# Prompt attention with 64-feature heads: key rows stacked in high and low parts, and scores in two passes in place of three

## What is computed

```python
# FoX: F is the running sum of the log forget gates
s = einsum('bqhd,bkhd->bhqk', q, k) * 64 ** -0.5
s = s + F_q[..., :, None] - F_k[..., None, :]
s = where(kpos <= qpos, s, NEG_INF)
y = einsum('bhqk,bkhd->bqhd', softmax(s), v)
# SWA: bands of two chunks, with ALiBi and a sink
s = einsum('bcqngd,bcknd->bcngqk', q, k) * 64 ** -0.5 - slopes * dist
y = sink_softmax(s, sink) @ v
```

## Time and profile before

| | us |
|---|---|
| median of 3 runs | 3229.61 (3228.44 to 3230.09) |
| the profiled execution | 3231.43 |
| its span, first to last instruction | 3229.7 |
| TensorE products busy | 2960.0 (92%) |
| TensorE weight loads busy | 2770.8 (86%) |
| VectorE busy | 1578.2 (49%) |
| ScalarE busy | 999.4 (31%) |
| GpSimd busy | 919.6 (28%) |
| mean granted TensorE clock | 0.938 of full speed |

### The profile page before, as it was taken

One profiled execution on the slowest core, in us unless ns is written; L12 is line 12 of the kernel. 1 busy time (PEld: TensorE's weight loads), 2 busy tenths in 40 slices (PEclk: granted clock), 3 DMA queues, 4 the chain that ended last, 5 costly groups with the idle time before them and its releaser, 6 DMA issues. The chain is left out here.

```text
span 3229.7 us, 51941 instructions
## 1 busy us (share of the span) xinstructions
PE 2960.0 (92%) x20656; PEld 2770.8 (86%) x20656; DVE 1578.2 (49%) x2747; ACT 999.4 (31%) x2259; POOL 919.6 (28%) x538
## 2 busy tenths in 40 slices
PE   6998877689999999999999998776899999999998
PEld 6997755379999999999999975645699999999998
DVE  3336555763344444444452574657443444444443
ACT  4334435553311111111243263455343111111111
POOL 3112134133422322322231123332243322223220
PEclk9998968798999999999999998787899999999999
DMA  5120100003411111111211201000133111111111
GB/s 162 39 68 23 40 11 18 1 14 100 153 40 52 46 45 39 52 39 42 69 65 38 77 2 41 11 18 1 34 120 126 52 39 39 52 39 52 39 52 55
DMA packets 181253, 161.86 MB, mean 50 GB/s; under 512 B 17236, under 2 KB 168316, under 8 KB 180860
## 3 DMA queue, kind: packets, MB, share of 16 engines
q1 hardware_dynamic: 181116, 160.02, 15.8%
HBM read 129.97 MB, written 30.13 MB: 50 GB/s over the span
## 5 line engine op out<-in xcount | busy, mean ns | idle before, releaser
L2059 PE MATMUL bank_b<-x_hi,fwhi 128*128 128x352 f32 x2112 | 689.3, 326 | 5.3 <-POOL fwlo L2015 5.3
L2059 PE MATMUL bank_b<-x_hi,fwlo 128*128 128x352 f32 x2112 | 687.5, 326 | 0.0
L2059 PE MATMUL bank_b<-f_lo,fwhi 128*128 128x352 f32 x2112 | 685.9, 325 | 0.0
L2015 POOL TENSOR_TENSOR fwlo<-raw,fwhi 128x1024 fp32r<-128x1024 f32 x132 | 321.8, 2438 | 578.7 <-ACT fwhi L2140 568.2
L2059 PEld LDWEIGHTS bank_b<-x_hi,fwhi 128*128 128x128 f32 x2112 | 398.8, 189 | 6.6 <-POOL fwlo L2015 5.9
L2059 PEld LDWEIGHTS bank_b<-f_lo,fwhi 128*128 128x128 f32 x2112 | 401.1, 190 | 0.0
L2059 PEld LDWEIGHTS bank_b<-x_hi,fwlo 128*128 128x128 f32 x2112 | 397.8, 188 | 0.6
L2248 DVE TENSOR_TENSOR fx<-fx,bank_b 128x352 f32<-128x352 f32 x528 | 275.8, 522 | 242.6 <-PE bank_b L2089 242.6
L2089 PE MATMUL bank_b<-fuhi,fwhi 128*128 128x352 f32 x1056 | 343.8, 326 | 4.5 <-DVE fulo L2242 4.5
L2089 PE MATMUL bank_b<-fulo,fwhi 128*128 128x352 f32 x1056 | 345.3, 327 | 0.0
L2089 PE MATMUL bank_b<-fuhi,fwlo 128*128 128x352 f32 x1056 | 344.7, 326 | 0.0
(11 more groups left out here) (428 smaller groups left out, 6025.6 us busy)
## 6 DMA issues: line engine op xcount, KB each, us to landing
raw<-in_w_ffn_up SPq DMA_DIRECT2D x88, 512.0 KB, 3.8
raw<-in_w_ffn_down SPq DMA_DIRECT2D x44, 512.0 KB, 3.5
wraw<-in_w_in SPq DMA_DIRECT2D x18, 984.0 KB, 5.4
xs<-x_between SPq DMA_DIRECT2D x16, 528.0 KB, 3.9
x_between<-xs SPq DMA_DIRECT2D x16, 528.0 KB, 2.7
fx<-x_between SPq DMA_DIRECT2D x2, 4224.0 KB, 12.5
raw<-in_w_out SPq DMA_DIRECT2D x16, 512.0 KB, 5.3
x_between<-fx SPq DMA_DIRECT2D x3, 1408.0 KB, 5.7
```

Source lines behind the costliest of these rows:

```text
L2015: pool.tensor_tensor(self.wlo[:, r], self.raw[:, o % 2], self.whi[:, r].bitcast(F32), ALU.subtract)\
L2059: last = pe.matmul(bank[:, first_bank + t, 0:TN], w[:, role, c, :], x[:, c, self.cols(t)], start=(c == 0 and m == 0), stop=(c == DC - 1 an ...
```

## The change

For 64-feature heads the high queries are stored twice, in rows 0 to 63 and 64 to 127 of `qT[0]`, and the keys' high part in rows 0 to 63 and low part in rows 64 to 127 of `kT[0]`. The first pass contracts over 128 rows: high query x high key plus high query x low key. The second takes the low queries with the high keys, over 64 rows in SWA and 66 in FoX. In FoX it needs the high keys a second time, in `kT[1]`, whose rows 64 and 65 take the high and low part of -F; rows 64 and 65 of the low queries are 1. ScalarE makes the extra copies: of the queries in both kinds, of the keys in FoX. The zero rows and their memsets and waits go; one GpSimd memset of ones stays in FoX. MLA (96 features) keeps three passes. In SWA `kT` has one array in place of two.

```diff
-        qT = [T("qT" + n, [96, RQ, 2, P], F32R) for n in ("hi", "lo")]
-        kT = [T("kT" + n, [96, 2, 2, SEQ], F32R) for n in ("hi", "lo")]
+        stacked = kdim == HD
+        rest = HD + 2 * fox
+        depth = (P, rest) if stacked else (kdim, kdim)
+        qT = [T("qT" + n, [d, RQ, 2, P], F32R) for n, d in zip(("hi", "lo"), depth)]
+        kT = [T("kT" + n, [P if stacked else kdim, 2, 2, SEQ], F32R) for n in ("hi", "lo")[0:1 if swa else 2]]
+        k_rest = kT[-1]
...
-                        if p == 1:
-                            sp.wait_ge(cleared, 5)
...
-                            if p == 0:
-                                sp.wait_ge((cleared, dve_cleared)[n], 1)
...
-                                sp.dma_start(kT[n][64:65, p % 2, e, :].bitcast(F32), frow[n][h:h + 1, :].bitcast(F32))\
-                                  .then_inc(row_in[p % 2], 16)
+                                sp.dma_start(k_rest[HD + n:HD + n + 1, p % 2, e, :].bitcast(F32),
+                                             frow[n][h:h + 1, :].bitcast(F32)).then_inc(row_in[p % 2], 16)
...
-                if kdim < 96:
-                    jobs = [(kT[0][64:96, 0], 0.0), (qT[0][64:96], 0.0)] + [(qT[0][64:65], 1.0)] * fox + \
-                           [(kT[0][64:96, 1], 0.0), (kT[1][64:96, 1], 0.0)]
-                    for n, (rows, value) in enumerate(jobs):
-                        pool.memset(rows.bitcast(F32), value).then_inc(cleared, 1)
-                        pool.wait_ge(cleared, n + 1)
+                if fox:
+                    pool.memset(qT[1][HD:rest].bitcast(F32), 1.0).then_inc(cleared, 1)
+                    pool.wait_ge(cleared, 1)
...
-                        if kdim < 96 and m == 0:
-                            pe.wait_ge(cleared, 2 + fox)
-                            pe.wait_ge(dve_cleared, 2)
-                        if kdim < 96 and r == QT:
-                            pe.wait_ge(cleared, 4 + fox)
+                        if fox and m == 0:
+                            pe.wait_ge(cleared, 1)
...
-                                for j, (x, y) in enumerate(((0, 0), (0, 1), (1, 0))):
-                                    last = pe.matmul(bank[:, 0:n], qT[x][:, r % RQ, e, :],
-                                                     kT[y][:, p % 2, e, f + a:f + a + n],
-                                                     start=(j == 0), stop=(j == 2 and not diag))
+                                passes = [(qT[0], kT[0], P), (qT[1], k_rest, rest)] if stacked else \
+                                    [(qT[x], kT[y], kdim) for x, y in ((0, 0), (0, 1), (1, 0))]
+                                for j, (q, kk, d) in enumerate(passes):
+                                    last = pe.matmul(bank[:, 0:n], q[0:d, r % RQ, e, :],
+                                                     kk[0:d, p % 2, e, f + a:f + a + n],
+                                                     start=(j == 0), stop=(j == len(passes) - 1 and not diag))
...
                     act.activation(qT[0][0:kdim, r % RQ, :, :], psX[0:kdim, 0], ACT.Copy)
-                    act.activation(kT[0][0:kdim, p % 2, :, i * P:(i + 1) * P], psX[0:kdim, 1], ACT.Copy)\
-                       .then_inc(x_hi, 1)
+                    last = act.activation(kT[0][0:kdim, p % 2, :, at], psX[0:kdim, 1], ACT.Copy)
+                    if stacked:
+                        last = act.activation(qT[0][HD:P, r % RQ, :, :], psX[0:HD, 0], ACT.Copy)
+                    if fox:
+                        last = act.activation(k_rest[0:HD, p % 2, :, at], psX[0:HD, 1], ACT.Copy)
+                    last.then_inc(x_hi, 1)
...
-                    dve.tensor_tensor(kT[1][0:kdim, p % 2, :, at], psX[0:kdim, 1],
-                                      kT[0][0:kdim, p % 2, :, at].bitcast(F32), ALU.subtract).then_inc(x_lo, 1)
-
-                if kdim < 96:
-                    dve.memset(kT[1][64:96, 0].bitcast(F32), 0.0).then_inc(dve_cleared, 1)
-                    dve.memset(qT[1][64:96].bitcast(F32), 0.0).then_inc(dve_cleared, 1)
+                    k_lo = kT[0][HD:P, p % 2, :, at] if stacked else kT[1][0:kdim, p % 2, :, at]
+                    dve.tensor_tensor(k_lo, psX[0:kdim, 1], kT[0][0:kdim, p % 2, :, at].bitcast(F32), ALU.subtract)\
+                       .then_inc(x_lo, 1)
```

More of the change, by code:

```diff
@@ L1018, in attend_prompt @@
     sink = 1 if swa else 0
-    with own_semaphores(nc, "att", "clr ld x xh xl s m e n t tl th o y d iv pn dc", [("row", 2)]) as sem, \
+    with own_semaphores(nc, "att", "clr ld x xh xl s m e n t tl th o y d iv pn", [("row", 2)]) as sem, \
             ExitStack() as s:
         T = lambda n, shape, dt=F32: s.enter_context(nc.sbuf_tensor(n + kind + k.tag, shape, dt))
-        qT = [T("qT" + n, [96, RQ, 2, P], F32R) for n in ("hi", "lo")]
-        kT = [T("kT" + n, [96, 2, 2, SEQ], F32R) for n in ("hi", "lo")]
+        stacked = kdim == HD
[4 more added lines that the diff above has]
+        k_rest = kT[-1]
         NPR = 3
@@ L1035, in attend_prompt @@
         (cleared, loaded, row_in, x_done, x_hi, x_lo, scored, maxed, expd, normed, turned, t_low, t_high, mixed,
-         y_done, dve_steps, inverted, pool_normed, dve_cleared) = (sem[n] for n in ("clr", "ld", "row", "x", "xh", "xl", "s", "m", "e", "n", "t", "tl",
-                                                "th", "o", "y", "d", "iv", "pn", "dc"))
+         y_done, dve_steps, inverted, pool_normed) = (sem[n] for n in ("clr", "ld", "row", "x", "xh", "xl", "s", "m", "e", "n", "t", "tl",
+                                                "th", "o", "y", "d", "iv", "pn"))
         ident = k.const[:, C_ID:C_ID + P]
@@ L1186, in high_part @@
                     act.wait_ge(x_done, r + 1)
+                    at = slice(i * P, (i + 1) * P)
                     act.activation(qT[0][0:kdim, r % RQ, :, :], psX[0:kdim, 0], ACT.Copy)
-                    act.activation(kT[0][0:kdim, p % 2, :, i * P:(i + 1) * P], psX[0:kdim, 1], ACT.Copy)\
-                       .then_inc(x_hi, 1)
+                    last = act.activation(kT[0][0:kdim, p % 2, :, at], psX[0:kdim, 1], ACT.Copy)
[4 more added lines that the diff above has]
+                    last.then_inc(x_hi, 1)
                 for r in range(AHEAD):
```

## The result

The changed kernel takes 3249.87 us (median of 6 runs, 3240.01 to 3255.2) against 3230.16 us (3228.44 to 3236.59) for the kernel before: ratio 1.0052, 95% interval 1.0038 to 1.0067. It is slower by 0.5%; forecast were 3210 us and a gain of 0.6%. The profiled execution took 3255.0 us, its span 3253.2, mean granted clock 0.931.

A forecast was written before the change was run, and what follows sets the result against it. The matmul engine, busy nine tenths of the span, was taken as the bound, with waits on other engines limiting gains. Per layer fox 7.9 and swa 1.9 us, twice: 19.6 off 3229.6 gives 3210.0 us; range 3197 to 3221.

The forecast's parts named there:

- rows cost nothing: the load of weights lies under the product in front of it in both: Score passes in fox and swa: 128, 66 or 64 rows for 96 add no time; weight loads stay hidden.
- The hold of 0.09 us per unit: VectorE's low key part starting at partition 64 loses overlap: 0.09 us per change, swa's VectorE turn 2.46 to 2.55.
- a margin of 0.06: Swa: ScalarE's added copy would end at 492.68, VectorE takes the low query part at 492.74, so just hidden.
- the start, costed as a gain of 0.8: Swa stage's start: gives 0.8 us, beside 1.1 in some 22 units, for 1.9 per layer.
- Fox's middle pair: Fox head pair: 2.54 of 4.4 us kept, less 0.2 for holds, gains 2.34; middle pair about 35.7 us for 38.0.
- i = 5 to 7: Fox pair's later units, one head at a time: 0.35 each at 5, 0.17 and 0.41 at 6, 0.1 and 0.46 at 7.
- i = 4, first head: Fox pair: 0.34 us lost, because the turning of probabilities waits for GpSimd's normalising, a chain that doesn't get shorter.
- Fox's start: First fox pair: 0.3 us left before the first score, about 0.8 from slow-clock units; start gain 1.1.
- the walk: Fox: waits followed through a middle head pair's twelve units, finding 2.54 of 4.4 us kept; the first pair lacks 0.24.
- ScalarE's copies become the path: Rival, chance 0.04: every fox and swa tile pays all its copies, 40 us against a gain of 20: 3250.
- The clock falls at pair borders: Rival, chance 0.10: longer waits at fox's head-pair borders bring half clock, two per stage, costing 7 us: 3217.
- longer steps at 128 rows: Sign in the profile after that would show the forecast wrong; expected were 0.23 us steps at 512 columns.

The follow-up runs named there:

- with 66 rows: Changed kernel, but swa's second pass contracts over 66 rows in place of 64, rows 64 and 65 of the low queries zero: 3229.59 us, ratio 0.9989.
- The copy alone: Kernel before, plus one ScalarE copy of the queries per swa tile to partitions 64 to 127 of an unread spare tile: 3234.99 us, ratio 1.0002.
- the low key part alone: Kernel before, but in swa VectorE's low key part goes to partitions 64 to 127 of a spare tile; scores read zeros instead: 3243.65 us, ratio 1.0038.
- the copies alone: Kernel before, plus two ScalarE copies per fox tile into an unread spare tile, queries to partition 64, keys to 0: 3237.92 us, ratio 1.0015.
- All on GpSimd: Changed kernel's fox with swa as before, but GpSimd makes all fox's second copies out of the first ones: 3221.06 us, ratio 0.9958.
- three passes of 64 rows: Kernel before, nothing stacked, but swa's three score passes read 64 rows in place of 96: 3248.03 us, ratio 1.0051.
- with 128: Changed kernel, but swa's second pass contracts over 128 rows in place of 64, low queries' rows 64 to 127 zero: 3227.1 us, ratio 0.9988.
- the best version: Changed kernel, but GpSimd makes the second copies in fox and swa and moves swa's low keys up; swa's second pass has 66 rows: 3213.98 us, ratio 0.9941.
- fox alone stacked: Fox from the changed kernel, swa from the kernel before: 3224.38 us, ratio 0.9977.

## Why the prediction was wrong

- **The step that failed** is "rows cost nothing: the load of weights lies under the product in front of it in both". It was read from 96 and 128 rows and carried over to 64, for which the trace of before has no score row. For fox's 66 rows it is right. For swa's 64 it is wrong: 0.31 us for 0.12. This and the half clock that lasts longer with it are 10.0 and 9.8 us in the two layers, 19.8 of the 28.6 us by which swa missed (+24.8 for -3.8).
- **The rule that bears on it** was not weighed. The Trainium skill (TensorEngine Tiling (Array Packing), Key Properties) says that changing the tiling mode, and not only the tile, drains the engine, and its section When to Use Tiling has row tiling as something to choose for contractions of up to 64 rows. It doesn't say that a plain product over 64 rows changes the mode by itself; that is inferred here. The traces fit: 0.19 us more per change between 128 rows and 64 at the full clock, 0.3 at the half, none at 66 rows. No trace shows such a step where only the columns of the weights change (128*64 to 128*128 turnings, 491.44 to 491.55 us in the kernel before: 0.11). The rule that the prediction did weigh (a load overlaps only into another row group) disagrees with the 0.12 steps at 66, 96 and 128 rows.
- **Swa without that** would still have been 2.4 and 2.7 us slower, not 1.9 faster. The hold of 0.09 us per unit was right (2.56 for the forecast 2.55). ScalarE's copy, costed at nothing by a margin of 0.06, is late by 0.08 a unit: the margin left out that ScalarE is held 0.1 us for its change of partition and that VectorE starts 0.03 us after ScalarE's end. Of this the loop pays only a little, 0.10 us in eight units. And the start, costed as a gain of 0.8, is a loss: 0.6 us is gained before the first score (6.8 for 7.4), but from there to the eighth unit's scores it takes 19.6 us with 66 rows for 17.4 and 17.1. The copy alone brings 0.5 and 0.9 of these 2.1 and 2.5 us, the low key part alone 0.9 and 0.4; the rest stays open.
- **Fox's middle pair**: 1.9 us for 2.34. The units with i = 1 and 3 kept what was forecast to 0.02 us, those with i = 5 to 7 together 1.6 for 1.8. The rest is mostly at i = 4, first head, which got 0.30 us longer (3.46 for 3.16) where nothing was put down: the turning there waits 0.64 us for VectorE's low key part and not, as the forecast had it, for GpSimd. ScalarE's copies with their hold are 0.2 us of it, shown by the copies alone.
- **Fox's start**, mis-sized: a forecast gain of 0.3 before the first score was a loss of 0.2, and the first pair gained 0.1 and 0.5 where 2.9 were put down (2.10 of the walk and 0.8 of the slow units). The walk took the middle pair's slack for the first pair's; there the chain through ScalarE is bare. All on GpSimd, 1.4 us before the first score and 2.3 to 2.4 in the first pair are kept. The two layers' misses in fox sum to 8 us.
- **Sum**: 3210 + 28.6 + 8 = 3247; measured 3250.
- **The rivals**: "ScalarE's copies become the path" gave 3250 with chance 0.04, and the number is right by accident: copies and holds explain at most what stays of swa's loss with 66 rows, 2.4 us of 12.4, and most of what fox lacks. "The clock falls at pair borders" did not happen inside a fox stage; the half clock that grew is the one at swa's start. No rival had the weight load; the sign "longer steps at 128 rows" named the kind of row that would show it, though not the height that causes it.

Open: why the half clock lasts longer was not tried by itself. The runs show how far it reaches into the swa stage, first and second layer: 15 and 14 us before, 29 and 29 after, 23 and 32 with three passes of 64 rows, 19 and 20 with 66 rows, 19 and 22 with 128. So it is longest with 64-row passes, but longer than before with 66 and 128 rows too, whose steps are 0.12.

## What to carry over

Before shortening a contraction, look at which heights stand next to each other in TensorE's list, and keep 64 rows from standing beside 128 (64, 66, 96 and 128 were measured): two rows of zeros cost nothing here and saved 20 us. A copy that is hidden in the middle of a stage can be bare in its first units, so walk the start by itself. Where GpSimd idles, it can make second copies from SBUF off the chain through psX.

## What the runs showed of the hardware

- Products of 64 and 128 rows in turn start 0.31 us apart at 256 columns and the full clock, 0.51 at the half; 66 and 128 rows: 0.12 and 0.21; 64 rows alone: 0.12.
- ScalarE, like VectorE, loses its overlap of 0.1 us when the output's start partition changes: copies of 64x256 start 0.26 us apart at one partition and 0.37 to 0.39 across a change.
- GpSimd's 64x256 copy from SBUF to SBUF takes 0.39 to 0.40 us in most cases (179 of 192 in the best version), about as long as ScalarE's 0.38 out of psX; single ones take up to 0.87.
- The granted clock near a stage's end falls to half in some executions of the same kernel and not in others; it is worth 1.4 to 1.6 us (fox alone stacked: 44.9 us without, 46.5 with).
